# Hybrid mixer of a two-layer decoder trunk, rewritten: delta rule in one chunk of 128 tokens per block, norms folded into scalars, inverse accumulated in PSUM

## What is computed

```python
p = h @ w_in                       # q k v z (512 each), b a (4 each), sc_b sc_c sc_h (512 each)
qkv = silu(causal_dwconv(concat[q, k, v], gdn_conv_w))
q, k = l2norm(q), l2norm(k)        # per head of 128
beta = sigmoid(b_raw);  g = -exp(a_log) * softplus(a_raw + dt_bias)
# S_t = a_t S_{t-1} + beta_t k_t (v_t - a_t S_{t-1}^T k_t)^T,  a_t = exp(g_t),  o_t = S_t^T q_t
o = gated_delta_chunked(q, k, v, beta, g)      # the reference uses chunks of 64
o = o * rsqrt(mean(o * o) + 1e-6) * out_norm * silu(z)
y_sc = sc_b * causal_dwconv(sc_c * sc_h, sc_conv_w)
return concat([o, y_sc]) @ w_out
```

## Time and profile before

| what | us |
|---|---|
| median of 3 runs (1054.97, 1070.25, 1076.26) | 1070.25 |
| the profiled execution | 1053.87 |
| its span | 1052.1 |
| PE busy of the span | 1015.6 |
| DVE busy | 648.1 |
| ACT busy | 468.5 |

### The profile page before, as it was taken

The page is one execution under the profiler, slowest core; times in us unless marked ns, Lnnn a source line. Parts: engine busy times, 40 slices in busy tenths (PEclk is TensorE's granted clock), DMA queues, the critical chain, the costliest instruction groups (busy, mean ns, idle before and its releaser), DMA issues.

```text
span 1052.1 us, 19776 instructions
## 1 busy us (share of the span) xinstructions
PE 1015.6 (97%) x8304; PEld 990.4 (94%) x8304; DVE 648.1 (62%) x694; ACT 468.5 (45%) x509; POOL 66.8 (6%) x56
## 2 busy tenths in 40 slices
PE   6999999988999999999999999999989999999997
PEld 5899999987999899999999999999988899999996
DVE  5655555789985247655556755545679557555553
ACT  5544443646324135444345544444646464444442
POOL 0100000100000001000000100000000001000000
PEclk9999999998999889999999999999999999999999
DMA  8666656543432116755655576565543125665651
GB/s 250 216 212 199 199 165 198 174 123 101 121 120 81 40 42 201 226 190 183 199 193 166 167 234 199 180 201 194 174 160 121 40 82 184 215 199 181 197 200 40
DMA packets 136035, 172.80 MB, mean 164 GB/s; under 512 B 4293, under 2 KB 123322, under 8 KB 135994
## 3 DMA queue, kind: packets, MB, share of 16 engines
q1 hardware_dynamic: 134176, 171.26, 50.5%
q10 hardware_dynamic: 1818, 0.96, 0.3%
HBM read 171.15 MB, written 1.05 MB: 164 GB/s over the span
## 4 chain that ended last, share of the span: by engine, by line
PE 84%; DVE 11%; ACT 3%; DMA 1%; issue 1%; POOL 0%; DVEq 0%; POOLq 0%; SPq 0%; ACTq 0%
PE bank L352 23%; PE bank L353 23%; PE bank L357 23%; PE bank L641 5%; DVE w_lo L330 3%; PE bank L1452 2%; DVE work L1287 1%; DMA raw<-in_ffn_w_up 1%; ACT w_hi L318 1%; PE bank L859 1%; PE bank L879 1%; PE bank L883 1%; PE bank L918 0%; DMA work<-in_x 0%; PE bank L1528 0%
## 5 line engine op out<-in xcount | busy, mean ns | idle before, releaser
L330 DVE TENSOR_TENSOR w_lo<-raw,w_hi 128x2048 fp32r<-128x2048 f32 x154 | 354.3, 2301 | 190.0 <-ACT w_hi L318 189.9
L352 PE MATMUL bank<-h_hi_rest,w_hi 128*128 128x256 f32 x1428 | 394.5, 278 | 0.7 <-DVE h_lo_rest L434 0.7
L353 PE MATMUL bank<-h_lo_rest,w_hi 128*128 128x256 f32 x1428 | 393.4, 277 | 0.0
L357 PE MATMUL bank<-h_hi_rest,w_lo 128*128 128x256 f32 x1428 | 385.8, 277 | 0.0
L318 ACT ACTIVATE w_hi<-raw 128x2048 fp32r<-128x2048 f32 x159 | 302.7, 1909 | 169.9 <-PE bank L357 149.5
L352 PEld LDWEIGHTS bank<-h_hi_rest,w_hi 128*128 128x128 f32 x1428 | 269.1, 188 | 1.3 <-DVE h_lo_rest L434 1.1
L353 PEld LDWEIGHTS bank<-h_lo_rest,w_hi 128*128 128x128 f32 x1428 | 268.9, 188 | 0.0
L357 PEld LDWEIGHTS bank<-h_hi_rest,w_lo 128*128 128x128 f32 x1428 | 264.9, 188 | 0.0
L352 PE MATMUL bank<-act_hi,w_hi 128*128 128x256 f32 x480 | 132.6, 276 | 1.2 <-DVE act_lo L585 1.2
L353 PE MATMUL bank<-act_lo,w_hi 128*128 128x256 f32 x480 | 132.5, 276 | 0.0
L357 PE MATMUL bank<-act_hi,w_lo 128*128 128x256 f32 x480 | 132.5, 276 | 0.0
(11 more groups left out here) (268 smaller groups left out, 1307.9 us busy)
## 6 DMA issues: line engine op xcount, KB each, us to landing
raw<-in_ffn_w_up SPq DMA_DIRECT2D x44, 1024.0 KB, 5.4
raw<-in_ffn_w_down SPq DMA_DIRECT2D x44, 1024.0 KB, 4.9
raw<-in_ffn_w_gate SPq DMA_DIRECT2D x43, 1024.0 KB, 5.4
raw<-in_hyb_w_in SPq DMA_DIRECT2D x14, 1024.0 KB, 5.3
raw<-in_swa_w_qkv SPq DMA_DIRECT2D x6, 1024.0 KB, 5.0
raw<-in_hyb_w_out SPq DMA_DIRECT2D x4, 1024.0 KB, 5.3
raw<-in_swa_w_o SPq DMA_DIRECT2D x4, 1024.0 KB, 5.3
work<-in_x SPq DMA_DIRECT2D x2, 512.0 KB, 5.5
```

What stands on the lines that cost most here:

```text
L330: nc.vector.tensor_tensor(w_lo[slot(ch)][:], raw[:, slot(ch), :], w_hi[slot(ch)][:].bitcast(F32), ALU.subtract).then_inc(lo_split, 1)
L352: nc.tensor.matmul(out_ap, w_hi[s][:, wcols], mv_hi, start=start, stop=False, skip_group_check=True)
L353: i = nc.tensor.matmul(out_ap, w_hi[s][:, wcols], mv_lo, start=False, stop=False, skip_group_check=True)
L357: return nc.tensor.matmul(out_ap, w_lo[s][:, wcols], mv_hi, start=False, stop=stop, skip_group_check=True)
```

## The change

The input chunks come in the order k c q v h b z, and the phases are placed anew:

```diff
-        HYB_COLS = [KEY, KEY + CW, 0, CW, SCC + 512, SCC + 512 + CW, 2 * KEY, 2 * KEY + CW, SCC + 1024,
-        KINDS = "kqcvhbz"
+        HYB_COLS = [KEY, KEY + CW, SCC + 512, SCC + 512 + CW, 0, CW, 2 * KEY, 2 * KEY + CW, SCC + 1024,
+        KINDS = "kcqvhbz"
+        HYB_BANKS = [GATE, UP, ACC[0], ACC[1]]
...
+        HYB_PLAN = {(0, 1): ["gates"], (2, 1): ["gates_turned"], (3, 1): ["gates_logged"], (4, 0): ["pairs"],
+                    (4, 1): ["decay"], (5, 0): ["first_inverse"], (5, 1): ["start"],
+                    (6, 0): ["left1"], (6, 1): ["right1"], (7, 0): ["left2"], (7, 1): ["right2"],
...
+                    (10, 0): ["left5"], (10, 1): ["right5"], (11, 0): ["last_left", "v_turn"],
+                    (11, 1): ["last_right", "k_turn"], (12, 0): ["attention", "solve0"],
+                    (12, 1): ["state", "out0"], (13, 0): ["correction", "o_sum0"], (13, 1): ["solve1"]}
```

```diff
+            if name == "pairs":
+                pe.wait_ge(hyb_evacuated, 4)
+                pe.wait_ge(kq_silu, 2)
...
+                        i = mm(head(ACC[b], h), tokens(k_t, b, h), tokens(k_t, b, h), start=True, stop=True)
...
+                        i = mm(ACC[2][:, n:n + 1], tokens(kq_sq, b, h), ones[:, 0:1], start=True, stop=True)
...
+        def hyb_pool(pool):
+            pool.wait_ge(sums_ready, 1)
+            nc.gpsimd.tensor_tensor(ty(T_SK), ty(T_S), ty(T_HALF), ALU.pow).then_inc(root_ready, 1)
```

The inverse and its transpose stay in PSUM in four banks and are added to there; ACT copies them out after each level, and DVE has no part in it. The masks hold -1, so that products add. Starting them takes 16 products with the identity. There is a sixth level for blocks of 64, on a quarter of each matrix:

```diff
             if name == "start":
-                pe.wait_ge(pairs_masked, 1)
...
+                        i = mm(head(ACC[2 + b], h), one(inv_t, b, h), ident, start=(h == 0), stop=False,
+                               skip_group_check=True)
...
+                        mm(head(ACC[b], h), ident, one(inv_t, b, h), start=(h == 0), stop=False,
...
+            if name == "last_left":
...
+                        i = mm((AUX, AUX2)[b][HI, h * 64:(h + 1) * 64], one(lower, b, h)[LO, HI],
...
+                for b in range(TB):
+                    act_e.wait_ge(inverse_added, TB * n + b + 1)
+                    a(by_pair(inv, b), bank_pair(ACC[2 + b]), ACT.Copy).then_inc(inverse_copied, 1)
```

The output projection has lost its recurrence phases; ACT takes block 1's squares behind the end of block 0:

```diff
             out_part(0, conv_tiles, [0], True)
-            hyb_tensor_phase(pe, "add1")
+            hyb_tensor_phase(pe, "out1")
             out_part(0, conv_tiles, [1], False)
-            hyb_tensor_phase(pe, "read2")
-            hyb_tensor_phase(pe, "o_sum0")
+            hyb_tensor_phase(pe, "o_row0")
+            hyb_tensor_phase(pe, "o_sum1")
...
             for b in range(TB):
...
-                load_table(ACT.Sqrt)
...
+                if b == 1:
+                    hyb_scalar_phase(act_e, "out1")
                 act_e.wait_ge(o_final, b + 1)
```

More of the change, by code:

```diff
@@ new lines, in hyb_tensor_phase @@
+            if name == "attention":
+                pe.wait_ge(v_scaled, 1)
+                pe.wait_ge(kq_silu, 4)
+                for b in range(TB):
+                    for h in range(HEADS):
+                        i = mm(head(ACC[2 + b], h), tokens(k_t, b, h), tokens(q_t, b, h), start=True, stop=True)
+                i.then_inc(pair_products, 1)
+            if name == "solve0":
+                pe.wait_ge(inverse_t_copied, TB * N_LEVEL)
+                for h in range(HEADS):
+                    i = mm(head(ACC[0], h), one(inv_t, 0, h), one(rhs, 0, h), start=True, stop=True)
+                i.then_inc(y_solved, 1)
@@ new lines, in hyb_tensor_phase @@
+            if name == "state":
+                pe.wait_ge(k_scaled, 1)
+                pe.wait_ge(y_copied, 1)
+                for h in range(HEADS):
+                    i = mm(head(ACC[1], h), head(k_g, h), one(y_tok, 0, h), start=True, stop=True)
+                i.then_inc(state_added, 1)
+            if name == "out0":
+                pe.wait_ge(pairs_masked, 2)
+                for h in range(HEADS):
+                    i = mm(head(ACC[2], h), one(y_tok, 0, h), one(attn, 0, h), start=True, stop=True)
+                i.then_inc(o_ready, 1)
@@ new lines, in hyb_tensor_phase @@
+            if name == "correction":
+                pe.wait_ge(state_ready, 1)
+                for h in range(HEADS):
+                    i = mm(head(ACC[0], h), tokens(k_t, 1, h), head(state, h), start=True, stop=True)
+                i.then_inc(state_read, 1)
+            if name == "solve1":
+                pe.wait_ge(qg_ready, 1)
+                for h in range(HEADS):
+                    mm(head(ACC[3], h), head(state, h), head(qg_t, h), start=(h == 0), stop=False,
+                       skip_group_check=True)
+                pe.wait_ge(rhs_ready, 1)
+                for h in range(HEADS):
+                    i = mm(head(ACC[1], h), one(inv_t, 1, h), one(rhs, 1, h), start=True, stop=True)
+                i.then_inc(y_solved, 1)
@@ L921, in hyb_tensor_phase @@
+            if name == "out1":
+                pe.wait_ge(y_copied, 2)
+                for h in range(HEADS):
+                    i = mm(head(ACC[3], h), one(y_tok, 1, h), one(attn, 1, h), start=False, stop=True,
+                           skip_group_check=True)
+                i.then_inc(o_ready, 1)
             if name[:5] == "o_sum":
@@ L930, in hyb_tensor_phase @@
                 pe.wait_ge(o_diagonal, b + 1)
[L931 removed]
+                mm(AUX[:], ones[:], o_diag[:, b * 512:(b + 1) * 512], start=True, stop=True) \
                   .then_inc(o_rows_ready, 1)
[L933 to L944 removed]
         def hyb_vector_phase(dve, name):
@@ L1114, in hyb_scalar_phase @@
+            if name == "correction":
+                dve.wait_ge(state_read, 1)
+                for h in range(HEADS):
+                    n = HEADS + h
+                    i = v.scalar_tensor_tensor(out=one(rhs, 1, h), in0=head(ACC[0], h),
+                                               scalar=tiny[:, T_NEGC, n:n + 1], in1=one(rhs, 1, h),
+                                               op0=ALU.mult, op1=ALU.add)
+                i.then_inc(rhs_ready, 1)
         def hyb_scalar_phase(act_e, name):
```

547 lines of the change are left out of this document (224 added, 323 removed), and 1 row of the table HYB_PLAN.

## The result

| | before | after |
|---|---|---|
| median of plain runs, us | 1062.61 (4 runs, 1050.67 to 1076.26) | 1038.83 (4 runs, 1037.14 to 1039.71) |
| profiled execution, us | 1053.87 | 1039.71 |
| its span, us | 1052.1 | 1037.9 |
| next stage's first matmul, us | 394.15 | 377.44 |

The ratio is 0.9865, with an interval from 0.9824 to 0.9907: 1.35% faster, the interval ending just short of 2%. The forecast was 1048 within 1031 to 1065, likeliest no change beyond 2%. The ratio leaves out before's two disturbed runs (1070.25 and 1076.26), so it is nearer to one than the two medians are, and it rests on two runs of before, 1050.67 and 1054.97. In later measurements before's median was 1050.86 (7 runs), 1052.22 (19) and 1051.75 (18); against the first of them the new kernel's 1038.83 is 12.0 us faster.

The account below looks back on a forecast made before the run. PE's stream of matmuls was taken to bound the kernel. 375.2 + 4 for clock + 0.8 for table gave a stage end of 380.0, 14.1 us less; 1039.8 profiled plus half of 16.4 made a median of 1048, range 1031 to 1065.

Parts of the forecast that it names:

- The sum for the stage: Mixer stage: 375.2 us at full clock, plus 4 for clock and 0.8 for table, ends at 380.0 against 394.15.
- the addition for the median: Whole kernel: half of the 16.4 us between before's median and profiled time, added to 1039.8, gives a median of 1048.
- The cause named for before's low end: Old output projection with recurrence between: low clock together with small products lengthens the end; clock loss there 8.7 us.
- Up to the first inverse: Early mixer: DVE's steps end at 248.7 us, PE waits 2.2, the start's 16 products take 3.56, to 252.3.
- Levels and last chunks: PE-bound: five levels at 10.87 us to 306.7, then chunks 11 to 13 at 12.2, 10.0 and 9.2, to 338.1.
- The output norm: Output projection: PE waits about 0.3 us for the first diagonal and 1.9 for `o_sum1`, behind ACT's squares.
- Two spells at 4 us: Mixer: of three weak places, two drop the clock to half speed, losing 4 us out of 0 to 6.
- the one-column run: Chunk 11's end: about 5 us of small records, named as one of three places where the clock might fall.
- The clock holds: Rival: none of the three weak places drops the clock; stage end 376.0, gain 18.2, median 1044; chance 0.18.
- hand-overs eat it: Rival: thin PE lead at `solve1` and three-engine block chains lose 7 or 8 us; gain about 6, 1056; chance 0.17.
- The slow rival: Clock falls in chunk 11's one-column run, stays down until `o_row1`; stage end near 408, median 1076; chance 0.07.
- The table: Next stage's start: square root's table must load before ACT's splits; 0.8 us taken, between 0 and 1.3.

Follow-up runs that it names:

- a_alt: New kernel plus three unused groups between output chunks, 4 products 128 wide and 4 pairs alternating 128 and 64 rows, 64 wide; 1057.6 us, ratio 1.0026.
- b_seq: Kernel before, recurrence steps 1 to 3 reordered: four products with 128 rows first, then four with 64; 1044.38 us, ratio 0.9925.
- a_narrow: New kernel plus three unused groups between output chunks, 4 products 128 wide and 8 products 64 wide, all with 128 rows; 1048.08 us, ratio 0.9964.
- a_sq: New kernel with ACT computing block 1's squares before it waits for block 0's gated product; 1034.92 us, ratio 0.984.
- a_tab: New kernel with the square root's table loaded behind the mixer's last silu, not at the next norm; 1037.64 us, ratio 0.9864.
- a_cols: New kernel plus 48 unused one-column records at the end of chunk 11; 1052.71 us, ratio 1.0002.
- a_inv: New kernel with DVE's steps to the first inverse put in front of chunk 4's weight split; 1038.52 us, ratio 0.988.

## Why the prediction was right, and where it was not

- **The sum for the stage held.** 380.0 was forecast and 377.44 came. In the profiled execution, for which the sum was made, 1039.8 stood against 1039.71. So close a hit owes something to terms that cancelled: the stage ended 2.6 earlier than forecast, and of its 16.7 us 2.5 did not arrive at the end (1.5 for the table, the rest in later stages, where the attention stage's clock was 0.95 instead of 0.97). And both profiled executions stood a little high: before's 1053.87 is 2 to 3 us above its later medians, and 1039.71 is the highest of the new kernel's four runs.
- **The failed term is the addition for the median.** "I add half the 16.4" made 1048 of 1039.8, from two of three runs of before that stood at 1070 and 1076. The new kernel's four runs lie within 2.6 us, the profiled one the highest of them, so the addition to it was -0.9. Of before's 44 later runs 11 stood between 1062 and 1076, while no run of any kernel built on the new one passed 1060.11. That spread belonged to before and was not a distance between profile and plain run that a changed kernel inherits. Whether the alternating products cause it is open: a_alt's runs also fall into two groups, near 1051 and 1059, and b_seq's nine runs lie within 2.9 us, but nothing was run that settles it.
- **The cause named for before's low end was half right.** The prediction had "a low clock together with small products", and priced a narrow record at 0.105 from line 918's x8 row in step 0, where products with 64 rows stand unmixed. In steps 1 to 3 they alternate with 128 rows and cost 0.18. a_narrow (small, unmixed: no low clock), a_alt (mixed: low), b_seq (same work, unmixed: 1.00) show that the order of these products, and not their size, makes both the price and the low clock; for the price it is the change of row count. Since the whole segment was taken from the trace as 55.2 us, the sum was not touched; the reading of where the gain lies was. In the traces the old kernel takes 55.2 us from the first output matmul to the stage end, with its products reordered 44.7, and the new kernel 38.4. So 10.5 of the 16.9 us between the first and the last are to be had by reordering alone; by plain runs it is 7.9 of about 12.
- **Up to the first inverse.** The first start product was forecast at 248.7 and came at 249.21, its wait 2.9 instead of 2.2. The start's 32 records took 5.2 instead of 3.56: one of the two low spells forecast stood here. It is not there in every execution: in a_sq and a_tab, behind the same hole, they took 3.6.
- **Levels and last chunks.** 10.87 a level with no wait, as forecast; the first output matmul at 339.05 instead of 338.1. The start's 1.7 and the later first product, 0.5, explain more than that; the 64-wide records at 0.067 instead of 0.105 (32 of them, 1.2 us) gave back some. That no subtraction "stood in PE's way before either" was wrong by the 1.1 us wait for line 1082; the sum, which counts PE's work anew, did not use it.
- **The output norm.** `o_sum1` waited 1.9 for ACT's squares, exactly the forecast, and a_sq shows the chain: ACT held the squares behind block 0. Of the diagonal's wait I had 0.3 and it was 0.8, because POOL's power on four columns took 1.02, not the 0.56 of one column:

```profile
236.84 1.65 POOL L1149 TENSOR_TENSOR tiny<-tiny 128x8 f32<-128x8 f32 x1 [49.12 <-DVE tiny L1025]
...
341.99 1.02 POOL L1153 TENSOR_TENSOR tiny<-tiny 128x4 f32<-128x4 f32 x1 [103.50 <-DVE tiny L1317]
```

- **The clock.** Two spells at 4 us were forecast; about 3 us were lost, at the start and behind the hole at `o_sum1`, both places named. The third, the one-column run, did not fall. "The clock holds" was the better description of the end after 362; "hand-overs eat it" did not come: no wait stood at `solve1`.
- **The slow rival** had its trigger right in kind and its size and persistence wrong (a_cols): 64 such records brought the low clock and 16 did not, and the dense products behind it did not leave the clock down.
- **The table** cost 1.5 against 0.8, above the 0 to 1.3 that I had given it. The Trainium skill (ScalarE: Activation LUTs, What ACT_TABLE_LOAD costs) counts a drain on top of the load and reaches 2.66 us; moving the load away gave 1.5 (a_tab, from the stage's end to the next norm), which is near the load's 1.28 alone and well under the 2.66 of the Trainium skill.

## What to carry to other kernels

Read a product's price in the stream in which it stands: before writing "small products", look at which row counts follow each other, and group products of one shape before anything is rewritten. Where PE is the bound, closing a hole of 2 us can be worth more than its length (3.9 in a_sq) or nearly nothing (0.3 in a_inv), so judge the fix by plain runs and not by the one spell that a profile shows. A spread that one kernel's runs have is no addition to another kernel's profiled time.

## What the hardware showed unexpectedly

- fp32 products with 128 and 64 rows in turn: 0.18 us a record at the full clock against 0.13 in groups of eight records (b_seq), about 0.15 for each change of the row count, and the clock behind them down to 0.77 (a_alt) or 0.57 (before).
- The low spell behind a hole is not the same from one execution to another. From 228 to 234, behind the same 2 us wait for the split, the clock was 0.72 in a_sq and 1.00 in the new kernel and in a_narrow, whose code up to there is the same. What decides it was not found.
- One-column fp32 records cost 0.105 us each, nearly as much as wide ones, and 64 in a row brought the clock to 0.62; products of 64 rows and 64 columns cost 0.067 a record, less than one-column ones.
- POOL's power on 128 partitions takes 0.56 for one column, 1.02 for four and 1.65 for eight: it is not a fixed cost.
